# First mixer of a hybrid transformer: squares on VectorE, query rotations between the query and key products, one weight slot ahead of the decays; squares of the norms added up by GpSimd

## What is computed

```python
def even_layer(h, ...):
    u = rmsnorm(h, norm_mix)
    proj = u @ w_in
    rw_cols, mla_cols = proj[..., :RW_COLS], proj[..., RW_COLS:]
    rw_prev = jnp.pad(rw_cols[:, :-1], ((0, 0), (1, 0), (0, 0)))
    rw_cols = rw_cols + shift_mu * (rw_prev - rw_cols)
    y_a = rwkv7_time_mix(*split_cols(rw_cols, RW_SIZES), ...)
    y_b = mla_attention(*split_cols(mla_cols, MLA_SIZES), ...)
    h = h + jnp.concatenate([y_a, y_b], axis=-1) @ w_out
    return h + swiglu(rmsnorm(h, norm_ffn), ffn_wg, ffn_wu, ffn_wd)

def rmsnorm(x, g, eps=NORM_EPS):
    xf = x.astype(jnp.float32)
    xf = xf * lax.rsqrt(jnp.mean(xf * xf, axis=-1, keepdims=True) + eps)
    return (xf * g.astype(jnp.float32)).astype(x.dtype)
...
    log_w = -jax.nn.softplus(-(w0 + jnp.tanh(w_down) @ w2)) - 0.5
    decay = jnp.exp(-jnp.exp(log_w))
    a = jax.nn.sigmoid(a0 + a_down @ a2)
    g = jax.nn.sigmoid(g_down) @ g2
...
def mla_attention(q_lat, kv_lat, k_rope, ...):
    q = to_heads(rmsnorm(q_lat, q_norm) @ w_uq, h)
    q_nope, q_pe = q[..., :MLA_NOPE], apply_rope(q[..., MLA_NOPE:], cos_r, sin_r)
    kv = to_heads(rmsnorm(kv_lat, kv_norm) @ w_ukv, h)
    k_nope, v = kv[..., :MLA_NOPE], kv[..., MLA_NOPE:]
    k_pe = apply_rope(k_rope[:, :, None, :], cos_r, sin_r)
```

## Time and profile before

| | |
|---|---|
| median of 3 runs | 1964.96 us |
| the profiled execution | 1963.63 us, its span 1961.7 us |
| TensorE (PE) busy | 1884.0 us, 96% |
| weight loads (PEld) | 1635.8 us, 83% |
| VectorE (DVE) | 1467.0 us, 75% |
| ACT | 1141.5 us, 58% |
| GpSimd (POOL) | 39.4 us, 2% |
| mean granted TensorE clock | 0.972 |

### The profile page before, as it was taken

How to read it: one execution, slowest core, us unless ns; L and a number is a source line. 1 busy time by engine, 2 the same in 40 slices (tenths; PEclk the granted TensorE clock), 3 DMA queues, 4 the chain that set the end, 5 groups by cost and what they waited for, 6 DMA issues and landing times.

```text
span 1961.7 us, 28126 instructions
## 1 busy us (share of the span) xinstructions
PE 1884.0 (96%) x11217; PEld 1635.8 (83%) x11217; DVE 1467.0 (75%) x1543; ACT 1141.5 (58%) x1239; POOL 39.4 (2%) x84
## 2 busy tenths in 40 slices
PE   7879999999999899999999999999999999899998
PEld 6758889999976788888888888888888887899997
DVE  4677746555644498988989889888898897697685
ACT  5532234334343476767767667677776776566653
POOL 0020000000012000000000000000000000000010
PEclk9999989999987799999999999999999999999999
DMA  7200034554420488988889889899898998443441
GB/s 323 86 1 1 1 129 172 182 183 174 149 87 1 188 361 341 369 349 348 359 335 374 352 347 353 343 368 356 340 368 328 371 355 331 181 146 134 156 146 43
DMA packets 64208, 467.44 MB, mean 238 GB/s; under 512 B 7248, under 2 KB 7376, under 8 KB 7888
## 3 DMA queue, kind: packets, MB, share of 16 engines
q1 hardware_dynamic: 64080, 465.66, 61.3%
HBM read 464.58 MB, written 1.05 MB: 237 GB/s over the span
## 4 chain that ended last, share of the span: by engine, by line
PE 87%; DVE 7%; ACT 3%; issue 2%; DMA 1%; POOL 0%; SPq 0%; DVEq 0%; ACTq 0%
PE bank L551 85%; PE bank L561 3%; DVE split_ring L1872 1%; ACT arena L1340 1%; ACT split_ring L1340 1%; DVE arena L1903 0%; ACT L1340 0%; DMA weight_ring<-w_dram 0%; DVE arena L2587 0%; DVE arena L1904 0%; ACT moe_pair_high L1340 0%; ACT operand_high L1340 0%; ACT late_high L1340 0%; POOL arena L2679 0%; DVE arena L1882 0%
## 5 line engine op out<-in xcount | busy, mean ns | idle before, releaser
L2433 DVE TENSOR_TENSOR moe_pair_low<-weight_ring,moe_pair_high 128x2048 fp32r<-128x2048 f32 x225 | 507.2, 2287 | 15.8 <-ACT moe_pair_high L1340 15.2
L1340 ACT ACTIVATE moe_pair_high<-weight_ring 128x2048 fp32r<-128x2048 f32 x225 | 427.0, 1917 | 39.1 <-DMA weight_ring<-w_dram 37.9
L551 PE MATMUL bank<-moe_pair_high,operand_high 128*128 128x512 f32 x896 | 353.6, 395 | 3.5 <-DVE operand_low L2440 2.5
L551 PE MATMUL bank<-moe_pair_high,operand_low 128*128 128x512 f32 x896 | 352.3, 393 | 0.0
L551 PE MATMUL bank<-moe_pair_low,operand_high 128*128 128x512 f32 x896 | 349.9, 391 | 0.0
L551 PE MATMUL bank<-operand_high,split_ring 128*128 128x256 f32 x1536 | 328.6, 287 | 8.5 <-DVE split_ring L1872 8.2
L1340 ACT ACTIVATE arena<-bank 128x256 f32<-128x256 f32 (+4 forms) x209 | 90.4, 440 | 362.1 <-PE bank L551 326.8
L551 PEld LDWEIGHTS bank<-operand_high,split_ring 128*128 128x128 f32 x1536 | 256.5, 192 | 11.9 <-DVE split_ring L1872 9.6
L551 PEld LDWEIGHTS bank<-moe_pair_high,operand_high 128*128 128x128 f32 x896 | 168.7, 188 | 39.0 <-issue 2.7
L551 PEld LDWEIGHTS bank<-moe_pair_high,operand_low 128*128 128x128 f32 x896 | 168.4, 188 | 38.1
L551 PEld LDWEIGHTS bank<-moe_pair_low,operand_high 128*128 128x128 f32 x896 | 168.8, 188 | 36.7
(11 more groups left out here) (313 smaller groups left out, 3201.0 us busy)
## 6 DMA issues: line engine op xcount, KB each, us to landing
weight_ring<-w_dram SPq DMA_DIRECT2D x381, 1024.0 KB, 6.9
arena<-w_dram SPq DMA_DIRECT2D x55, 1024.0 KB, 4.9
constants<-const_dram SPq DMA_DIRECT2D x1, 3124.0 KB, 18.0
parameters<-param_dram SPq DMA_DIRECT2D x1, 2896.5 KB, 24.4
hT<-x_dram SPq DMA_DIRECT2D x1, 1024.0 KB, 4.9
out_dram<-squares SPq DMA_DIRECT2D x4, 256.0 KB, 2.1
constants<-const_dram SPq DMA_DIRECT2D x1, 128.0 KB, 4.7
parameters<-param_dram SPq DMA_DIRECT2D x1, 54.5 KB, 4.6
```

The lines of the kernel that those rows point to most:

```text
L551: return pe.matmul(out, lhsT, rhs, start=start, stop=stop, skip_group_check=True)
L1340: return act.activation(out, in_, f, **kw)
L2433: tt(low_, raw_, high_.bitcast(F32), ALU.subtract).then_inc(moe_split, 1)
```

## The change

1. The residual gets a semaphore of its own, and VectorE squares it, a piece of 128x512 at a time, before the parameters are waited for. ACT runs one small copy first, so that its table is loaded before the inputs land, and squares nothing there.
2. TensorE makes product 2 ahead of the LoRA matmuls. ACT copies weight 2 ahead of the first token shift, and weight 4 right behind weight 3. VectorE takes slot 2's `mix_in`, split 4 and the shift's sum ahead of the decays.
3. The four rotation products stand between the query products and the first key product; each waits for ACT's evacuation of its query pair. VectorE rotates three pairs, adds the first key pair, rotates the last, adds three. The product `Bs` and the two bonus products move into the first steps of the attention.
4. The block of level 0 is made before the turned form, and TensorE waits for the turned form only ahead of its second group.
5. For six sums of squares (that of the opening and the router's are left as they are), GpSimd adds pieces 1, 2 and 3 to piece 0, and TensorE adds the two chunks of piece 0 by two matmuls. At the end GpSimd adds two pieces, and TensorE takes the last one directly: four matmuls.

```diff
+            def sums_of_sums(bank, src, n, rest=()):
+                pe.wait_ge(S["sq_sum"], n)
+                chunks_ = (0, 1) + tuple(rest)
+                for i, c in enumerate(chunks_):
+                    if i == 2:
+                        pe.wait_ge(S["sq_piece"], 32)
+                    last = mm(bank[:, 0:T], C("ones"), src[:, c * T:(c + 1) * T], start=(i == 0), stop=(i == len(chunks_) - 1))
+                return last
...
             project(V)
             project(V)
+            project(V)
             pe.wait_ge(tables_loaded, 32)
-            pe.wait_ge(S["lora_in"], 2)
-            for w, x in ((Pm("wa2"), lw), (Pm("wa2"), lx), (Pm("g2"), sg)):
+            for w, x, inputs in ((Pm("wa2"), lw, 2), (Pm("wa2"), lx, 2), (Pm("g2"), sg, 3)):
+                pe.wait_ge(S["lora_in"], inputs)
                 for j2 in range(2):
...
+            def partners(j2, evacuated):
+                pe.wait_ge(A.freed, evacuated)
+                bank = V.claim(pe)
+                V.fill(mm(bank[:, :], C("partner_mla"), qh[:, 2 * j2:2 * j2 + 2, :]))
...
                 queries = A.fill(last)
+                if j2:
+                    partners(j2 - 1, queries - 1)
...
-                V.fill(last)
+                keys = V.fill(last)
+                if j2 == 0:
+                    partners(NH // 2 - 1, queries)
...
-            for j2 in range(2):
-                bank = V.claim(pe)
-                V.fill(mm(bank[:, 0:512], C("same_head"), sq_[:, 1024 + j2 * 512:1024 + (j2 + 1) * 512]))
-            pe.wait_ge(A.freed, queries)
-            rope(qh, NH, "mla")
             pe.wait_ge(S["rope_done"], 1 + NH // 2)
+            pe.wait_ge(V.freed, keys)
+            def bonus(i):
+                if i in (0, 2):
+                    at = 1024 + i * 256
+                    bank = V.claim(pe)
+                    V.fill(mm(bank[:, 0:512], C("same_head"), sq_[:, at:at + 512]))
             def mla_scores(h, bank):
                 mm(bank[:, 0:P], qh[:, h, 0:P], kh[:, h, 0:P])
...
-            attention(mla_scores, vml, 0)
+            attention(mla_scores, vml, 0, bonus)
...
-                pe.wait_ge(S["first_inverse"], a + 1)
+                if a:
+                    pe.wait_ge(S["first_inverse"], 2)
...
+                    if a == 0 and n == 0:
+                        pe.wait_ge(S["first_inverse"], 1)
...
-                        sums(banks[3], squares_low, 4).then_inc(S["std_ready"], 1)
+                        sums_of_sums(banks[3], squares_low, 3).then_inc(S["std_ready"], 1)
...
-            A.fill(sums(bank, sq_, 8))
+            A.fill(sums_of_sums(bank, sq_, 6))
...
-                A.fill(sums(bank, squares_low, 16 + 8 * l))
+                A.fill(sums_of_sums(bank, squares_low, 9 + 6 * l))
...
-                    A.fill(sums(bank, sq_, 20))
+                    A.fill(sums_of_sums(bank, sq_, 12))
...
-            A.fill(sums(bank, squares_low, 28))
+            A.fill(sums_of_sums(bank, squares_low, 17, (6, 7)))
...
-            act.wait_ge(loaded, 48)
+            st.lone(a_(tiny[:, 153:154], zcol, ACT.Copy))
+            act.wait_ge(x_landed, 16)
+            act.wait_ge(loaded, 32)
             for n in range(4):
                 h_parts(0, n)
-            for n in range(4):
-                h_squares(0, n, sq_)
             hi(0)
             done["norm", 0] = h_std(inv0)
             hi(1)
+            hi(2)
             act.wait_ge(S["mix_ready"], 1)
...
             lerped(6, 0)
-            hi(2)
             act.wait_ge(S["lerp_out"], 1)
+            st.say(a_(lx[HD:P], rw_dl[HD:P, 0, :], ACT.Copy), "lora_in")
             st.say(a_(lw[0:HD], rw_dl[0:HD, 0, :], ACT.Tanh), "lora_in")
-            st.lone(a_(lx[HD:P], rw_dl[HD:P, 0, :], ACT.Copy))
-            st.settle()
             st.say(a_(sg, rw_dl[:, 1, :], ACT.Sigmoid), "lora_in")
...
             hi(3)
+            hi(4)
             lerped(3, 2)
-            hi(4)
...
-            dve.wait_ge(loaded, 48)
+            dve.wait_ge(x_landed, 16)
+            for n in range(4):
+                cols = slice(2 * n * T, (2 * n + 2) * T)
+                st.say(tt(sq_[:, cols], hT_[:, cols], hT_[:, cols], ALU.mult), "sq_piece")
+            dve.wait_ge(loaded, 32)
...
             mix_in(0)
+            lo(2)
             lerped(6, 0)
-            lo(2)
             mix_in(1)
             lo(3)
             lerped(2, 1)
+            mix_in(2)
+            lo(4)
+            lerped(3, 2)
             dve.wait_ge(A.freed, done["lora", "w0"])
...
             st.own(tt(cs8, cs8, mid.rearrange("p (n o) -> p n o", o=1).broadcast_to([P, 8, P]), ALU.subtract))
-            mix_in(2)
-            lo(4)
-            lerped(3, 2)
             st.lone(tt(csx, cs, logd, ALU.subtract))
...
-            for j2 in range(NH // 2):
+            mla_tables = C("cos_mla"), C("sin_mla")
+            def keys_in(j2):
                 bank = V.take(dve)
                 V.free(tt(kh[:, 2 * j2:2 * j2 + 2, :], bank[:, :].rearrange("p (c t) -> p c t", c=2), kpe2, ALU.add))
-            dve.wait_ge(S["exp_out"], 1)
-            st.own(tt(Bs, kk, iclr, ALU.mult))
-            dve.wait_ge(A.freed, done["v_turned"])
-            for j2 in range(2):
-                bank = V.take(dve)
-                v2 = rw_v[:, 2 * j2:2 * j2 + 2, :]
-                V.free(tt(v2, v2, bank[:, :].rearrange("p (c t) -> p c t", c=2), ALU.mult))
-            rope(qh, NH, (C("cos_mla"), C("sin_mla")), rt1, rt2)
+            st.wait_said("lerp_out")
+            rope(qh, NH - 2, mla_tables, rt1, rt2)
+            keys_in(0)
+            rope(qh, NH, mla_tables, rt1, rt2, first=NH - 2)
+            for j2 in range(1, NH // 2):
+                keys_in(j2)
             v4 = lambda x: x.rearrange("p c (a t) -> p c a t", a=TT)
             def keys(i):
...
             def keys(i):
-                if i == 1:
+                if i in (0, 2):
+                    if i == 0:
+                        dve.wait_ge(A.freed, done["v_turned"])
+                    bank = V.take(dve)
+                    v2 = rw_v[:, i:i + 2, :]
+                    V.free(tt(v2, v2, bank[:, :].rearrange("p (c t) -> p c t", c=2), ALU.mult))
+                elif i == 1:
+                    dve.wait_ge(S["exp_out"], 1)
+                    st.own(tt(Bs, kk, iclr, ALU.mult))
+                elif i == 3:
                     st.own(tt(Bs, Bs, E3, ALU.mult))
-                elif i == 3:
+                elif i == 4:
                     st.own(tt(KR[:, :, :, 0, :], v4(kk), v4(E2), ALU.mult))
                 elif i == 5:
                     st.own(tt(KR[:, :, :, 1, :], v4(r_), v4(E1), ALU.mult))
...
             first_level()
+            level_block(0, 0)
             first_turned(0)
-            level_block(0, 0)
...
+            def normalized(heads):
+                for n in heads:
+                    i = n % NH
+                    L_ = late_Lg[i] if n >= 3 * NH else Lg[i % NL]
+                    pool.wait_ge(S["rz_ready"], n + 1)
+                    st.lone(pool.tensor_scalar(L_[:, 0:P], L_[:, 0:P], rz[:, i, 0:1], 1.0, ALU.mult, ALU.mult))
+                    st.say(pool.tensor_scalar(L_[:, P:384], L_[:, P:384], rz[:, i, 1:2], 1.0, ALU.mult, ALU.mult), "prob_ready")
+            def squares_added(src, piece, last=4):
+                for n in range(1, last):
+                    pool.wait_ge(S["sq_piece"], piece + n + 1)
+                    st.say(pool.tensor_tensor(src[:, 0:2 * T], src[:, 0:2 * T], src[:, 2 * n * T:(2 * n + 2) * T], ALU.add), "sq_sum")
+                    st.wait_said("sq_sum")
+            normalized(range(0, NH))
+            squares_added(squares_low, 4)
+            squares_added(sq_, 8)
+            normalized(range(NH, 3 * NH))
+            squares_added(squares_low, 16)
+            squares_added(sq_, 20)
+            normalized(range(3 * NH, 4 * NH))
+            squares_added(squares_low, 24)
+            normalized(range(4 * NH, 5 * NH))
+            squares_added(squares_low, 28, 3)
...
-            sp.dma_start(hT_[:, :], x_dram).then_inc(loaded, 16)
+            sp.dma_start(hT_[:, :], x_dram).then_inc(x_landed, 16)
```

16 lines of the change are left out of this document (5 added, 11 removed).

## The result

Four executions of the changed kernel have a median of 1947.52 us (1943.26 to 1949.75), those of the kernel before 1964.59 us. The ratio is 0.9907, its 95% interval 0.989 to 0.9924: 17.1 us faster, where 15.65 were forecast (1949.3 us), and inside the range. Measured again on another chip it took 1945.84 us, ratio 0.9900 (0.9882 to 0.9918).

What follows compares the result with a forecast made beforehand. TensorE, busy 96% of the span, was taken to bound the kernel. The mixer's 8.3 us and the norms' 7.35 made 15.65 us, giving 1949.3 us against the median; its own range was 1946 to 1953.

Steps and rivals of the forecast that it cites:

- five milestones: Product 0 starts at 14.85 us, split 7 ends 71.9, first logits 112.0, attention ends 134.0; mixer gains 8.3 us.
- forecast as 3.0, 2.6 and 2.9: Mixer: interleaved queries and keys gain 3.0 us, steps moved into attention cost 2.6, the solve's first level gains 2.9.
- ACT's queries and not 3.0: Queries and keys: TensorE makes two query pairs by 94.7 us, then waits 3.0 us for ACT's first query copy.
- product 0 starts 3.0 us early: Opening: early table load and squares on VectorE let product 0 start at 14.85 us, 3.0 us early.
- its 5.1: Opening and order of products: split 7 ends at 71.9 us and not 77.0, 5.1 us early.
- split to 294.0, last add to 295.4: Feed-forward norm: last GpSimd add follows the split, sums end at 296.4 against 297.0, gaining 0.6 us.
- the first rival: Norms: adds slip between VectorE's operations and all sums are saved: +2.1, +0.7, +4.0 us, 1942.5 us; chance 0.13.
- 2.0 forecast: Second mixer's norm: split to 488.1, last add to 489.5, sums end at 490.4 against 492.4, gaining 2.0 us.
- a sign of being wrong: Ahead of the second mixer: TensorE waiting over 1 us for GpSimd would show the forecast wrong.
- the sum of -1.3 and 2.7: Late layer 0: one vector's sums lose 1.3 us behind three adds, the other vector's gain 2.7 us.
- The add's price: Norms: one GpSimd add of 128x512 with two inputs takes 1.4 us, midway between 0.96 and 1.92.
- 7.35 forecast: Norms in all: 0.6, 2.0, -1.3, 2.7, 2.7 and 0.65 us at the end gain 7.35 us.

Runs made afterwards that it cites:

- both mends: Changed kernel with ACT's weight 3 copy ahead of the LoRA evacuation and late layer 0's first sum at eight TensorE matmuls: 1941.98 us, ratio 0.9882.
- the norms alone: Kernel before with only GpSimd's adds of squares and the short sums: 1955.27 us, ratio 0.9952.

## Why the prediction was right, and where it wasn't

**Right in the whole and in the mixer.** Its five milestones (14.85, 71.9, 112.0, 134.0, and 8.3 us for the mixer) came at 14.77, 72.12, 112.15, 133.92 and 8.26. The sum was made on lists of work for one engine at a time, with durations from rows, and the waits came out of these lists. The order of events bears the lists out: split 4 right behind split 3, the second group behind the first inverse. Between the traces before and after, the interleaved queries are worth 3.0 us, the steps moved into the attention cost 2.4, and the first level is worth 2.8, forecast as 3.0, 2.6 and 2.9; undoing each part alone bears this out, apart from the clock's falls.

That each milestone was met within 0.2 us is in part luck. The forecast had the first three products at full clock; in the profiled execution they were not, and those in which they were end split 7 at 70.4 to 71.1, about 1 us before the forecast. Taken over the five profiles with the mixer as changed, the events behind the solve stand 8.25, 5.86, 7.97, 9.26 and 5.82 us earlier than before, 7.4 in the mean; 8.3 lies inside this scatter, and the first profile happened to lie upon it. And TensorE waited 0.57 us for ACT's queries and not 3.0, since product 8 had taken 8.5 us and not 5.9; the logits came at the forecast time because ACT and VectorE set the pace there. Where product 8 ran as forecast, 3.0 us were lost (the run with both mends).

**Opening and order: right together, wrong apart.** The step "product 0 starts 3.0 us early", carried to split 7 as a share of its 5.1, fails: alone it gives 0.8 to 1.3 there, since TensorE waits for the LoRA weights until 29.79 (some 0.6 us) and runs the matmuls behind the wait at the lower clock (1.7 us). The forecast of the two together was safe from it because three products end at 32.

**Feed-forward: "split to 294.0, last add to 295.4" was the wrong order.** The first two adds ran in VectorE's gaps, and the third began at 283.40, 0.17 us ahead of the split at 283.57. The split was held up in its stead (3.38 us, not 2.29). 2.5 us were won, not 0.6, and 2.5 to 2.6 in all ten profiles with these adds. Ordering the adds behind the splits was a rule taken from one row. That is the first rival, at this one place.

**Second mixer: 2.0 forecast, 1.9 in the first profile, by another way.** The forecast had the last add behind the split; there all three were through before it. Where the third ran beside the split, as in seven profiles of ten, TensorE waited 1.1 us, which the forecast had named as a sign of being wrong, and 0.8 us were won. The right number was luck.

**Late layer 0: the sum of -1.3 and 2.7 left the clock out.** TensorE waited 3.28 us, and with the lower clock behind it the place came to -0.9 and not 1.4, 2.3 us less. Where the wait was 1.9 us it gave 3.0 behind the product. The forecast had looked at the clock in the mixer, where VectorE mostly hides it, and not here.

**The add's price was right.** 1.4 us were taken between 0.96 and 1.92. The groups by form of the changed kernel (columns: count, busy us, mean ns):

```profile
L2732 POOL TENSOR_TENSOR arena<-arena 128x512 f32<-128x512 f32 x11 | 20.3, 1848 | 1293.2 <-ACT arena L1369 1293.1
...
L2732 POOL TENSOR_TENSOR squares<-squares 128x512 f32<-128x512 f32 x6 | 8.1, 1356 | 187.6 <-ACT squares L1369 187.2
```

The mean of 1848 ns holds those beside splits; beside nothing one took 1.26 to 1.45 us. The Trainium skill (GPSIMD Engine Reference, Engine selection) warned that two-input work is about twice as slow there. It is, against VectorE's 0.69 us for the same shape, and the estimate from its figure was 1.1. It didn't speak against the change after all: GpSimd was busy for only 2% of the span before, and the sums taken off TensorE were worth more than the waits and longer splits. The same page (Specifications) says that GpSimd shares its SBUF interfaces with VectorE and that two SBUF inputs contend; 3.20 us beside a split and the split's 3.38 agree.

The feed-forward's surplus and late layer 0's deficit cancel: 6.8 us for the norms in the two traces, 7.35 forecast; in the profile of the norms alone it is 5.8. That the whole came within 1.8 us owes something to that, and to the clock.

## What to carry over

Write each engine's list with times beside it, and let the waits come out of the lists. Ask of every landing and every release how near it is behind the one that shows, since moving work earlier uncovers it. Give a wait of TensorE two prices, its own length and what the lower clock costs behind it, and put the second down only where no other engine sets the pace. Where a part is worth less than the clock's scatter, read its events in the trace and not the time of the whole, and read them in several profiles: one can show an order that the others don't have.
